# The sample's time mixing moved from the head of the program into the stream of expert gathers

## What is computed

```python
def step(S, inp):                       # layer 0: 16 heads of 64
    r_t, d_t, k_t, v_t, kk_t, a_t = inp
    Skk = jnp.einsum('bhvk,bhk->bhv', S, kk_t)
    S = (S * d_t[:, :, None, :] - Skk[..., None] * (kk_t * a_t)[:, :, None, :]
         + v_t[..., None] * k_t[:, :, None, :])
    return S, jnp.einsum('bhvk,bhk->bhv', S, r_t)
...
x = layer_norm(DN_ALPHA * x + mix, ...)  # behind each mixer
...
u = expert_u[eidx]                       # PEER: 8 heads x 16 experts a row
h = jax.nn.gelu(jnp.einsum('nhkd,nd->nhk', u, xr))
out = jnp.einsum('nhk,nhkd->nd', gate * h, expert_v[eidx])
x = layer_norm(DN_ALPHA * x + ffn, ...)
```

## Time and profile before

| | |
|---|---|
| median of 3 runs | 3441.63 us (3441.5 to 3451.39) |
| profiled execution | 3457.56 us, of which the span is 3455.8 us |
| PE, DVE, ACT, POOL busy | 2238.4, 1752.7, 674.4, 1040.0 us (65, 51, 20 and 30%) |
| moved by DMA | 1015.35 MB: 825.84 MB in POOL's queue, 187.39 MB in SP's |
| first gather issued | 997.0 us after the start |
| granted TensorE clock | 0.81 of full speed in the mean |

### The profile page before, as it was taken

The page is one execution under the profiler, slowest core; times in us unless marked ns, Lnnn a source line. Parts: engine busy times, 40 slices in busy tenths (PEclk is TensorE's granted clock), DMA queues, the critical chain, the costliest instruction groups (busy, mean ns, idle before and its releaser), DMA issues. The chain is left out here.

```text
span 3455.8 us, 33139 instructions
## 1 busy us (share of the span) xinstructions
PE 2238.4 (65%) x11761; PEld 1239.6 (36%) x11761; DVE 1752.7 (51%) x4053; ACT 674.4 (20%) x1892; POOL 1040.0 (30%) x985
## 2 busy tenths in 40 slices
PE   7949495785765554866668656675666665555555
PEld 3427384672742222332333223422333342222221
DVE  1143534423447776356445784466435348755555
ACT  1022121220111112133121331211222111211111
POOL 0013031310024444234333243232212234444442
PEclk9979697887888777868889778997888797787877
DMA  5220203012559999999999879998977989999998
GB/s 179 85 110 1 74 1 98 5 31 112 174 226 420 392 414 372 423 367 383 412 387 423 325 286 418 364 422 337 367 310 300 378 326 420 400 414 421 420 420 336
DMA packets 168899, 1015.35 MB, mean 294 GB/s; under 512 B 35360, under 2 KB 36176, under 8 KB 55072
## 3 DMA queue, kind: packets, MB, share of 16 engines
q0 software_dynamic: 117024, 825.84, 59.5%
q1 hardware_dynamic: 51712, 187.39, 14.4%
HBM read 987.99 MB, written 18.91 MB: 291 GB/s over the span
## 5 line engine op out<-in xcount | busy, mean ns | idle before, releaser
L1352 PE MATMUL fl_acc<-fl_pairs,fl_diag 128*64 128x512 f32 x3072 | 1070.9, 785 | 788.4 <-ACT fl_diag L1320 788.4
L1376 POOL DMA_INDIRECT fl_pairs<-in_peer_uv,fl_row_at x768 | 863.8, 1125 | 1526.3 <-PE fl_acc L1352 1393.1
L1299 DVE CUSTOM_DVE_ANT_0 fl_pairs<-fl_pairs,fl_rows 128x1024 f32<-128x1024 f32 x768 | 925.7, 1222 | 486.3 <-DMA fl_pairs<-in_peer_uv,fl_row_at 485.7
L1352 PEld LDWEIGHTS fl_acc<-fl_pairs,fl_diag 128*64 128x64 f32 x3072 | 426.1, 168 | 1335.0 <-issue 1249.1
L1328 ACT ACTIVATE fl_acts<-fl_dots 128x2 f32<-128x2 f32 x384 | 78.1, 204 | 1156.8 <-DVE fl_dots L1299 1156.5
L1320 ACT ACTIVATE fl_diag<-constants_sb,fl_mix 128x64 f32<-128x64 f32 x768 | 224.6, 340 | 342.2 <-DVE fl_mix L1289 341.0
L1289 DVE TENSOR_TENSOR fl_mix<-fl_row_gate,fl_acts 128x2 f32<-128x2 f32 x384 | 59.0, 155 | 250.3 <-ACT fl_acts L1328 209.1
L1736 PE MATMUL aacc<-aw_ring,at_xT 128*128 128x512 f32 x288 | 141.1, 632 | 7.6 <-DMA aw_ring<-in_kvq_by_pair 7.6
L284 PE MATMUL acc<-w_ring,mixed 128*128 128x512 f32 x288 | 127.2, 604 | 10.0 <-issue 9.1
L1448 PE MATMUL pbank_late<-at_yT,wq_late 128*128 128x128 f32 x768 | 99.8, 291 | 27.5 <-DMA wq_late<-in_query_by_head 27.5
L1448 PEld LDWEIGHTS pbank_late<-at_yT,wq_late 128*128 128x128 f32 x768 | 94.6, 204 | 50.3 <-DMA wq_late<-in_query_by_head 40.6
(11 more groups left out here) (374 smaller groups left out, 2743.3 us busy)
## 6 DMA issues: line engine op xcount, KB each, us to landing
aw_ring<-in_kvq_by_pair SPq DMA_DIRECT2D x36, 1024.0 KB, 9.4
wq_late<-in_query_by_head SPq DMA_DIRECT2D x24, 1024.0 KB, 9.5
fl_pairs<-in_query_by_head SPq DMA_DIRECT2D x16, 1024.0 KB, 5.0
cache_k<-in_past_k SPq DMA_DIRECT2D x16, 1024.0 KB, 11.9
cache_v<-in_past_v SPq DMA_DIRECT2D x16, 1024.0 KB, 9.8
w_ring<-in_rwkv_w_rkv SPq DMA_DIRECT2D x24, 512.0 KB, 3.3
fl_pairs<-in_peer_uv,fl_row_at POOLq DMA_INDIRECT x768, 16.7
pt_w_o<-in_out_by_pair SPq DMA_DIRECT2D x12, 1024.0 KB, 17.1
```

The costliest lines, as they stand in the source:

```text
L1299: dve.tensor_tensor_reduce(pair, pair, self.rows[:, u % 2, j, :], 1.0, 0.0, ALU.mult, ALU.add, self.dots[:, u % 2, q, j:j + 1]).then_inc(* ...
L1352: mm = pe.matmul(self.acc[j * FOLD:(j + 1) * FOLD, half, :], self.diag[:, self.summed % self.DIAGS, j, :], self.ring[:, g % self.RING, D + ...
L1376: pool.indirect_dma_start(self.ring[:, self.gathered % self.RING, :], None, self.io["peer_uv"], bass.IndirectOffsetOnAxis(ap=self.row_at[: ...
```

## The change

The head now ends with the two prompt tiles: the loop over tiles, `load_rows`, `to_features` and `project_and_norm` take `TILES - 1`. The sample's time mixing becomes `mixing_tile`, which stands between `open_flow` (now 38 turns) and `attention_tile(0)` and takes the flow along for 78 turns. It works in two halves of eight heads. `half_operands` (8 ticks), `half_chunks` (35 ticks: groups of two heads, five rounds of seven ticks) and `half_outputs` (13 ticks) do what `wkv_operands`, `wkv_chunks`, `wkv_states` and `wkv_outputs` did for the tile, with tiles half as wide, and each starts with loads of its own from the spill. Then the gated rows are turned, projected and normalized (`turn_features`, `project_tile` with the layer's weights), turned again, and scored (`key_scores`). The host passes the sample's states already turned (`states_turned`), and the states that go out are turned by the host, so the turning on chip is gone, for the prompt's too.

To make room in SBUF two of the ring's ten places are a buffer of their own (`fl_more`), which is closed during `mixing_tile`: the gathers 68 to 223 (the turns 34 to 111) have eight places. `open_flow` scores tile 1 alone; it no longer borrows two places of the ring for the query weights. The choice of use 2 moves behind the mixing, into the first stages of `attention_tile(0)`, and the later stages have new turn numbers: each use's choice is now ended in the key, value and query projections (or, for use 5, in the first `run_flow`).

```diff
@@ class Flow @@
-    RING, DIAGS = 10, 3
+    PLACES, KEPT, DIAGS = 10, 8, 3
+    NARROW = range(68, 224)
...
+        for g in range(2 * TILES * SLOTS):
+            p = min(range(self.KEPT if g in self.NARROW else self.PLACES), key=lambda i: -1 if last[i] is None else last[i])
...
-        while self.gathered < min(self.due(n - 1) * GROUPS + self.RING, self.known * SLOTS):
+        while self.gathered < self.known * SLOTS:
+            g = self.gathered
+            if self.before[g] is not None and self.before[g] >= self.due(n - 1) * GROUPS:
+                break
@@ open_flow @@
-                flow.turns = ((1, 33, 40), (2, 65, 0))
+                flow.turns = ((1, 33, 37),)
@@ new @@
+def mixing_tile(core, io, flow, t, carry, at):
...
+        flow.close_extra()
+        for part in range(2):
+            with ExitStack() as of_half:
+                x = HalfTile(core, of_half, t, part)
...
+                half_operands(core, io, flow, x, last, **events)
...
+                half_chunks(core, flow, x, last, **events)
...
+                half_outputs(core, io, flow, x, carry, gated, last, **events)
+        flow.open_extra()
...
+            turn_features(core, flow, [([gated[:]], mixT)], f"mt_g{t}", last, **events)
...
+            project_tile(core, io, flow, mixT, io["mix_by_pair"], 0, t, last, **events)
...
+        turn_features(core, flow, [([core.x_tok[:, t, :]], xT)], f"mt_x{t}", last, **events)
...
+        key_scores(core, io, flow, xT, flow.choice, 0, t, last, **events)
@@ half_operands: loads of one half @@
+                sp.dma_start(z[:], core.spill["w"][x.t][:, x.cols]).then_inc(*z_in.by(16))
...
+                sp.dma_start(vec[:].rearrange("p i n -> p (i n)"), io["rwkv_vectors"][x.part:x.part + 1, :].broadcast_to([P, 3 * HALF])).then_inc(*vec_in.by(16))
@@ program @@
-            for t in range(TILES):
+            for t in range(TILES - 1):
@@ experts_and_attention @@
-        open_flow(core, io, flow, xT, choice)
+        open_flow(core, io, flow, xT, choice, 38)
+    mixing_tile(core, io, flow, 2, None, [
+        (43, {}), (63, {}), (71, {}), (76, {}), (96, {}), (104, {}), (105, {}), (110, {}), (111, {}), (116, {})])
...
-            (69, dict(turn=((2, 0, 3),), rows=((2, 1),))), (71, {}), (86, {}), (90, {}), (102, {}), (106, {}), (115, {}), (118, {}), (130, {})])
+            (118, dict(rows=((2, 1),), choose=2, side=20)), (119, dict(side=20)), (125, dict(side=110, end=23, turn=((2, 26, 29),))), (130, {}), (138, {}), (142, {}), (152, {}), (154, {}), (166, {})])
...
-            (133, dict(rows=((3, 1),))), (135, {}), (152, dict(u=3, side=75)), (156, dict(side=20)), (168, dict(side=50, end=8)),
-            (171, dict(turn=((3, 1, 0),))), (180, dict(turn=((3, 0, 2),))), (182, {}), (194, {})])
+            (169, dict(rows=((3, 1),), choose=3, side=15)), (170, dict(side=15)), (185, dict(side=120, end=24, turn=((3, 27, 29),))), (190, {}), (202, {}),
+            (206, {}), (215, {}), (217, {}), (229, {})])
...
-        (197, dict(rows=((4, 1),))), (199, dict(u=4, side=15)), (216, dict(side=110)), (221, dict(side=25, end=12, turn=((4, 15, 0),))), (240, dict(turn=((4, 0, 4),))),
-        (243, {}), (250, {}), (252, {}), (262, {})])
-    run_flow(core, flow, 32, 294, u=5, side=160, end=28, rows=((5, 1),), turn=((5, 31, 0),))
-    ffn_norm(core, io, flow, 3, 298)
-    run_flow(core, flow, 30, 328, turn=((5, 0, 4),))
+        (232, dict(rows=((4, 1),), choose=4, side=15)), (234, dict(side=15)), (250, dict(side=120, end=24, turn=((4, 27, 29),))), (255, {}), (273, {}),
+        (276, {}), (284, {}), (286, {}), (296, {})])
+    run_flow(core, flow, 24, 318, choose=5, side=160, end=20, rows=((5, 1),), turn=((5, 23, 0),))
+    ffn_norm(core, io, flow, 3, 322, turn=((5, 0, 1),))
+    run_flow(core, flow, 8, 330)
```

## The result

The changed kernel is slower: 3482.9 us in the median of five runs (3472.4 to 3487.7) against 3447.8 for the kernel before, measured with it (3441.5 to 3451.4). The ratio is 1.0097, with a 95% interval of 1.0082 to 1.0113. The forecast was 3356 us, in a range of 3290 to 3440. The profiled execution has a span of 3480.2 us. Except for the experiments with one run, only runs in the faster of the chip's two states are compared, and among them one kernel's times still differ by up to 0.9%.

The account below looks back on a forecast made before the run. A head without gathers, then a flow bound by DMA. Terms 767 + 206 + 533 + 375 + 419 + 584 + 487 = 3371 us, 85 under the span of 3455.8; 3441.6 - 85 = 3356 us, range 3290 to 3440.

Parts of the forecast that it names:

- The head: Before the first gather: losing the sample's mixing and smaller work saves 230 us, so the first gather comes at 767.
- the choice of use 0: End of the head: it holds the first gather until 989.6 us and was taken to stay.
- The output projection: In the head: a third of its 43.5 us on PE goes, 14.5 us.
- The turned states of the prompt: In the head: a third of two transpositions and of one load goes, estimated at 6 us together.
- `half_chunks`: Chunk stage of each mixing half, 20 turns: 100.5 us of PE work plus 16 of waits, 117 us; bounds 101 and 168.
- The slower rival: In half_chunks: a round's chain doesn't shrink for two heads, 168 us a half, 3458 in all; chance 0.12.
- The lock: In half_chunks: DVE dots and POOL expansions exclude each other, adding 30 us, 3386 in all; chance 0.10.
- The ring of eight: Gathers in the mixing: eight places suffice, nothing charged; as a rival, places held too long give 3402 us, chance 0.15.
- The sign that the prediction named: In the mixing: POOL waiting for PE with under 8 us from issue to landing would show the ring as cause.
- `half_outputs`: Output stage of each mixing half, 8 turns: 47 us of DMA plus excess 4, 51 us, between 47 and 60.
- `key_scores`: Scores at the end of the mixing: PE needs about 46 us with 5 turns, against 45 of DMA.
- The later stages: Behind the mixing: tile 0 takes 375 us, tile 1 419, tile 2 584, the end 487.

Follow-up runs that it names:

- all three edits: Changed kernel with gate product and diagonals in the tick of the dots, half_chunks turns packed into its first 20 ticks, expansions on DVE: 3400.9 us, ratio 0.9858.
- both first edits: Changed kernel with gate product and diagonals in the tick of the dots, and POOL's expansions cut to two of 64 columns: 3409.6 us (one run).
- Six places: Changed kernel with six ring places instead of eight for gathers 68 to 223: 3479.7 us (one run).
- these repairs: Changed kernel, gate product and diagonals in the dots' tick in mixing and attention, half_chunks and half_outputs packed, expansions on DVE: 3350.4 us, ratio 0.9720.
- the one edit of these: Kernel before, with gate product and diagonals in the tick of the dots from the end of open_flow on: 3421.7 us, ratio 0.9928.

## Why the prediction was wrong, point by point

**The head: right, and larger than said.** The first gather came at 752.5 us, forecast 767. Of the 14.5 us more, the step "the choice of use 0, which holds the first gather until 989.6, stays" was wrong. The DVE step that ends the choice, in the kernel before and after:

```profile
988.36 0.29 DVE L1215 TENSOR_REDUCE ch_norm<-fl_gate 128x8 f32<-128x128 f32 x1 [21.70 <-ACT fl_gate L1210]
```

```profile
744.42 0.28 DVE L1154 TENSOR_REDUCE ch_norm<-fl_gate 128x8 f32<-128x128 f32 x1 [0.43 <-ACT fl_gate L1149]
```

In the kernel before it waited 21.7 us for an exponential on ACT that was queued behind the copies of the scores of two other tiles; now there is one other tile, and the wait is gone. The output projection took 30.3 us on PE in place of 43.5, so it gave 13.3 us instead of 14.5. The turned states of the prompt gave nothing: what was at 580.6 us before, the end of the prompt's mixing, is now at 581.9.

**`half_chunks`: the term that failed, +94 us.** The step was: 50.5 us of chunk work and 50 of turns on PE, plus 16 for waits, "because PE was busy 90% of that stage, so work more than waiting set its time". That row showed the chunks without a flow. It could say what the chunks' chain costs by itself, and did: 71.5 us for a half, 13 above PE's work. It could say nothing of what happens when a second chain of four engines is put into the same in-order queues. The excess over PE's work is 165.2 - 100.5 = 65 us, not 16: PE was idle 50.6 us, and its own work took 114.6 us instead of 100.5. By the runs, in the first half: the gate product and diagonals behind the tile's waits, 24 us; the lock, 21 us; turns in alternate ticks, 19 us when packed alone. These overlap: the first two give 40 together, and with all three edits 37 are gained, the expansions then being on DVE. PE's longer work went with the waits: at a granted clock of 0.83 a turn took 2.9 us instead of 2.5, and with both first edits, at 0.95, 2.3 (45.7 us of `fl_acc` products in 20 turns). Of those 40 us, 23 were idle time of PE and 17 its own work. What stays above the forecast, 8 to 11 us, is waiting and not work: with both edits PE was busy 97.8 us, less than the 100.5 forecast, and idle 27.6, 20 of them before the flow's products, for the diagonals. The chunks alone left it idle 13.4, near the 16 of the sum. What still holds up the diagonals there is open.

**The slower rival: near the number, the mechanism wrong.** It gave 168 us a half and 3458 in all, and the point from which it decides, 4.6 us a tick; measured were 165 and 163, 3483 and 4.72. That it came nearer than the forecast was luck. The test named for it held (PE busy 69%, under 70). But its cause, a round that doesn't shrink, is refuted by the 71.5 us. Something in the profile did speak for a slow stage: the stages with hand-offs in each tick that spoke for it, 6.3 and 8.1 us a tick, had a flow in them; the row that spoke against it had none.

**The lock: real, and mis-sized.** It was to add 30 us in the whole kernel; cutting the expansions down gave 21.0 us a half, 38 us of span. The prediction charged it as a rival with 0.10 when each of its conditions was in the kernel's code, and left it out of the sum.

**The ring of eight: right, but its test was bad.** Six places cost nothing measurable. The sign that the prediction named, POOL's wait for PE with under 8 us from issue to landing, was there (94.3 us of wait, gathers of 7.5 us in the median of the first `half_chunks`) and meant the reverse: places came free late because turns were slow. The sign that tells them apart is the idle time before the dots, 0.0.

**`half_outputs`, +14 us each: mis-sized.** 4 us of excess were charged for a chain of eight state steps; it was 18 in both halves. Packing the turns, on top of the three edits, brought the stage to 53.

**`key_scores`, 67.2 us, about 15 over what was allowed.** PE needed 50.2 us, close to the 46 taken; the rest are mostly waits, 11.7 us for the query weights and 7.0 for the diagonals. (The prediction speaks of five short stages behind the halves; there are four, and its sum has four.)

**The later stages: mostly right.** Tile 1's attention took 61.6 us ("near 70"), tile 2's stages gained more than said, since `sample_attention` fell from 219.6 to 191.8 us, and the end came 10 us under. Tile 0 was 19 over: its projections took 79.4 us, 75 forecast. DMA's share in tile 0 is 0.85; that its first stages have too few turns for their length is the likely reason for the other 15, but no run separates it. The gap in the dots at turn 320 was 15.4 us where the turns stand 5 apart, 10 more, forecast 8; at turn 128 the gathers paused 20.6 us from start to start, but pairs that had landed covered it (dots at 1761.4 and 1768.6), forecast 12.

## What to carry to other kernels

Before work is woven into another stage's ticks, draw one tick with every engine's queue, and ask of each small step of the guest whether it stands behind a wait of the host: a gate product of 0.2 us and two diagonals of 0.6 together, in the wrong place, cost 24 us in 165. A stage's busy share measured without the guest says nothing on this. Spread evenly is not neutral: guest work in consecutive ticks can overlap itself, in alternate ticks it did not (20 turns took 146 us in consecutive ticks, 165 spread evenly). Where a mover moves work beside two-input DVE instructions, look for POOL instructions that read SBUF, and put their lock into the sum. With these repairs the change is worth having: 3350 us, 2.8% under the kernel before, while the one edit of these that was tried on the kernel before gave it 0.7%. Against that one, 3422 us, the gain is 2.1%.

## What the runs showed of the hardware

- The hold of POOL on DVE reaches the smallest instructions: a gate product of 128x2, 0.16 us by itself, took 1.33 us when a POOL copy of 0.30 us and an expansion of 1.04 us ran one behind the other beside it. Where a dot was running when an expansion was started, the expansion took 1.43 us instead of 1.04, and the dot behind it 2.05 instead of 1.22:

```profile
1045.11 2.05 DVE L1262 CUSTOM_DVE_ANT_0 fl_pairs<-fl_pairs,fl_rows 128x1024 f32<-128x1024 f32 x1
```

```profile
1044.66 1.43 POOL L2753 TENSOR_TENSOR hc_K_by_chunk<-hw_K_end,constants_sb 128x512 f32<-128x512 f32 x1
```

- Where PE waited more, its own work took longer. In `half_outputs` of the changed kernel the granted clock was 0.63 in the mean; the turn above, before which PE had idled 3.3 us, had 0.50 and took 3.88 us for its eight passes. With packed turns the mean was 0.79; the turns with 0.9 and 0.3 us of idle time before them had 1.00 and took 2.14. The two are the lower and the upper level of the clock, 1.2 and 2.4 GHz.
